# Inversion on diagonal blocks of 64, attention products in halves of 64, and products of constants in TensorE's waits

## The reference, cut to what matters

```python
for layer in range(DEPTH):
    h = rms_norm(x, mix_norm[layer])
    c_rwkv, c_dil, c_mla, c_hgrn = split_cols(h @ w_in[layer], MIXER_COLS)
    y_a = rwkv7_time_mix(c_rwkv, ...)
    y_b = dilated_attention(...)
    y_c = mla_attention(...)
    y_d = hgrn2_mixer(...)
    x = x + jnp.concatenate([y_a, y_b, y_c, y_d], axis=-1) @ w_out[layer]
    h = rms_norm(x, ffn_norm[layer])
    x = x + (swiglu(h, ...) if layer % 2 == 0 else moe_swiglu(h, ...))
return rms_norm(x, final_norm)
```

```python
def step(state, inp):
    r_t, w_t, k_t, v_t, kk_t, a_t = inp
    s_kk = jnp.einsum('bhvk,bhk->bhv', state, kk_t)
    state = (state * w_t[:, :, None, :] - s_kk[..., None] * (kk_t * a_t)[:, :, None, :]
             + v_t[..., None] * k_t[:, :, None, :])
    return state, jnp.einsum('bhvk,bhk->bhv', state, r_t)
```

## Time and profile before

| | us |
|---|---|
| median of 3 runs | 1707.56 (1707.05 to 1708.32) |
| profiled execution | 1705.68 |
| its span, first to last instruction | 1704.1 |
| mean granted TensorE clock | 0.973 of full |
| TensorE busy | 1594.8 (94%) |
| VectorE busy | 1321.5 (78%) |
| ScalarE busy | 1046.3 (61%) |
| GpSimd busy | 147.6 (9%) |
| HBM read and written | 432.54 MB and 23.59 MB, 268 GB/s over the span |

### The profile page before, as it was taken

How to read it: one execution, slowest core, us unless ns; L and a number is a source line. 1 busy time by engine, 2 the same in 40 slices (tenths; PEclk the granted TensorE clock), 3 DMA queues, 4 the chain that set the end, 5 groups by cost and what they waited for, 6 DMA issues and landing times.

```text
span 1704.1 us, 25728 instructions
## 1 busy us (share of the span) xinstructions
PE 1594.8 (94%) x9284; PEld 1373.5 (81%) x9284; DVE 1321.5 (78%) x1204; ACT 1046.3 (61%) x1032; POOL 147.6 (9%) x154
## 2 busy tenths in 40 slices
PE   6888978999897898799999999999999999999997
PEld 6877868999796787778888888888888888888776
DVE  4888555444457875578888898888888888888997
ACT  4634344343444344467777777777777777777775
POOL 1152100000003320000000000000000000000720
PEclk9989998999998999799999999999999999999999
DMA  6429035553242200679999999999999999999992
GB/s 240 162 78 406 27 154 192 179 188 125 74 149 90 75 1 1 265 281 371 382 378 373 364 398 370 376 387 370 385 376 372 389 372 381 381 373 363 401 357 120
DMA packets 67974, 456.88 MB, mean 268 GB/s; under 512 B 7264, under 2 KB 8448, under 8 KB 16464
## 3 DMA queue, kind: packets, MB, share of 16 engines
q1 hardware_dynamic: 59696, 425.28, 64.9%
q0 software_dynamic: 8080, 30.84, 4.7%
q10 hardware_dynamic: 144, 0.05, 0.0%
HBM read 432.54 MB, written 23.59 MB: 268 GB/s over the span
## 4 chain that ended last, share of the span: by engine, by line
PE 78%; DVE 12%; issue 5%; ACT 4%; DMA 0%; DVEq 0%; SPq 0%; ACTq 0%
PE bank L383 32%; PE bank L408 16%; PE bank L1173 8%; PE bank L386 8%; PE bank L636 6%; PE bank L412 4%; DVE wl L458 2%; ACT wh L454 1%; PE bank L668 1%; PE bank L396 1%; DVE ml L623 1%; DVE hs L1927 1%; PE bank L1178 1%; DVE rw L1827 1%; PE bank L1485 1%
## 5 line engine op out<-in xcount | busy, mean ns | idle before, releaser
L458 DVE TENSOR_TENSOR wl<-ring,wh 128x2048 fp32r<-128x2048 f32 x369 | 853.9, 2317 | 181.0 <-ACT wh L454 177.5
L454 ACT ACTIVATE wh<-ring 128x2048 fp32r<-128x2048 f32 x369 | 705.6, 1914 | 120.2 <-PE bank L408 48.8
L383 PE MATMUL bank<-wh,xh 128*128 128x512 f32 x896 | 359.7, 401 | 4.5 <-DVE wl L458 3.0
L383 PE MATMUL bank<-wh,xl 128*128 128x512 f32 x896 | 350.6, 391 | 0.0
L383 PE MATMUL bank<-wl,xh 128*128 128x512 f32 x896 | 349.2, 390 | 0.0
L383 PEld LDWEIGHTS bank<-wh,xh 128*128 128x128 f32 x896 | 168.2, 188 | 37.4 <-DVE wl L458 3.7
L383 PEld LDWEIGHTS bank<-wh,xl 128*128 128x128 f32 x896 | 168.1, 188 | 37.2
L383 PEld LDWEIGHTS bank<-wl,xh 128*128 128x128 f32 x896 | 168.7, 188 | 32.5
L408 PE MATMUL bank<-wh,gh 128*128 128x512 f32 x448 | 176.2, 393 | 5.9 <-DVE gl L531 5.9
L408 PE MATMUL bank<-wl,gh 128*128 128x512 f32 x448 | 175.0, 391 | 0.0
L408 PE MATMUL bank<-wh,gl 128*128 128x512 f32 x448 | 174.9, 390 | 0.0
(11 more groups left out here) (320 smaller groups left out, 2482.1 us busy)
## 6 DMA issues: line engine op xcount, KB each, us to landing
ring<-in_moe_w SPq DMA_DIRECT2D x336, 1024.0 KB, 5.0
ring<-in_ffn_w SPq DMA_DIRECT2D x33, 1024.0 KB, 4.7
ring<-in_w_in SPq DMA_DIRECT2D x24, 1024.0 KB, 4.9
ring<-in_w_out SPq DMA_DIRECT2D x8, 1024.0 KB, 4.7
job_x<-xrow POOLq DMA_DIRECT2D x1, 8192.0 KB, 27.7
job_y<-xrow POOLq DMA_DIRECT2D x1, 8192.0 KB, 46.3
xrow<-job_x POOLq DMA_DIRECT2D x7, 512.0 KB, 9.6
job_y<-yj POOLq DMA_DIRECT2D x7, 512.0 KB, 4.7
```

Source lines behind the costliest of these rows:

```text
L383: ins = nc.tensor.matmul(up_bank(run, par, 0)[:], x[:, 0:C], w[b][:, k], **kw)
L454: nc.scalar.activation(wh[:, buf], flat_slot(slot), ACT.Copy).then_inc(sem("w_high"), 1)
L458: nc.vector.tensor_tensor(wl[:, buf], flat_slot(run.place(i)[0]), wh[:, buf].bitcast(F32), ALU.subtract).then_inc(sem("w_split"), 1)
```

## The change

`BLOCKS` = 6 levels now work on diagonal blocks of `H` = 64 and the last level joins them. A block constant `blocks` (two masks of 64 columns and six level masks, stacked for both diagonal blocks) is loaded on SyncE's queue behind unit 5, in both layers, and counted by `const_in`. The first score set is computed as 24 products of 64x64 instead of 8: the two diagonal blocks of each matrix side by side in the first 256 columns of a bank, the block above the diagonal in the next. VectorE masks the diagonal ones into `atd` and copies the others to `ato`. All tiles of the inversion (`xin`, `xit`, `mtd`, `pid`) are 128x256 per half in place of 128x512; each product of a matrix becomes two of 64x64x64. The transposes into `xin` become products with the identity. In level 6 only X0^T (A01 X1)-like products are left: 4 + 4 per half. Its result goes, negated, to the upper rows of `xit`, and the upper diagonal block is kept in `xi0`. `solve` takes two products a head.

`attend` writes its output in two halves of 64 partitions: 6 products in place of 3. `spin(b, n)` puts n products of the constant `ones` with 256 columns of constants into bank b, whose result nobody reads.

```diff
+        def spin(b, n):
+            for _ in range(n):
+                nc.tensor.matmul(bank[b][:, 0:T], cst("ones"), const[:, 0:T], start=True, stop=True)
...
+                    if u == 5:
+                        sp.dma_start(blocks[:].rearrange("p a b -> p (a b)"), A["blocks"]).then_inc(sem("const_in"), 16)
...
-                for l in range(1, LEVELS):
+                for l in range(1, BLOCKS):
...
-                        settle(nc.gpsimd.tensor_tensor(mtm[:, hv], atm[:, hv], over(lvl(l), 4), ALU.mult), "level_masked")
+                        settle(nc.gpsimd.tensor_tensor(mtd[:, hv], atd[:, hv], over(blocks[:, 2 + l], 4), ALU.mult),
+                               "level_masked")
...
+                        if n == 0:
+                            for to, at, (k0, i0) in ((0, 0, (0, 0)), (H, 0, (H, H)), (0, T, (0, H))):
+                                for half in range(2):
+                                    h, c = 2 * (m // 2) + half, m % 2
+                                    lo, hi, j = rows(h)
+                                    mm(bank[bk + half][to:to + H, at + m * H:at + (m + 1) * H],
+                                       a[lo:hi, j, c * P + k0:c * P + k0 + H], b[lo:hi, j, c * P + i0:c * P + i0 + H],
+                                       sig="chunk_ready" if m == 3 and at and half else None)
+                            continue
...
-                    mm(first, pts[:, n % 2, 0:P], v[:, 0])
-                    mm(second, pts[:, n % 2, P:T], v[:, 0], True, False)
-                    mm(second, pts[:, n % 2, T:3 * P], v[:, 1], False, True, "attended")
+                    for q in (0, P // 2):
+                        mm(first[q:q + P // 2], pts[:, n % 2, q:q + P // 2], v[:, 0])
+                    for q in (0, P // 2):
+                        mm(second[q:q + P // 2], pts[:, n % 2, P + q:P + q + P // 2], v[:, 0], True, False)
+                        mm(second[q:q + P // 2], pts[:, n % 2, T + q:T + q + P // 2], v[:, 1], False, True,
+                           "attended" if q else None)
...
+                DIAGONAL = tuple((m, r, slice(r * H, r * H + H)) for m in range(4) for r in range(2))
...
-                        for m in range(4):
-                            mm(bank[2 + half][:, m * P:(m + 1) * P], mtm[:, 4 * half + m], xin[:, 4 * half + m],
-                               sig="mx_ready" if m == 3 else None)
+                        for m, r, d in DIAGONAL:
+                            if not last:
+                                mm(of_block(bank[2 + half][d], m), mtd[d, 4 * half + m], xin[d, 4 * half + m],
+                                   sig="mx_ready" if m == 3 and r else None)
+                            elif r:
+                                mm(of_block(bank[2 + half][d], m), ato[0:H, 4 * half + m], xin[0:H, 4 * half + m],
+                                   sig="mx_ready" if m == 3 else None)
...
                         beside(l, half)
+                        if last:
+                            spin(4, 1)
...
-                        mm(bank[6][:, h * HD:(h + 1) * HD], xit[:, mat(h, c)], rsol[:, h],
-                           sig="u_ready" if h == NH - 1 else None)
+                        o, m = bank[6][:, h * HD:(h + 1) * HD], mat(h, c)
+                        mm(o[0:H], xi0[0:H, m], rsol[0:H, h])
+                        mm(o[H:P], xit[:, m], rsol[:, h], sig="u_ready" if h == NH - 1 else None)
```

More of the change, by code:

```diff
@@ L144, in constants, with block_constants @@
     return c
+def block_constants():
+    i = np.arange(P)[:, None] % H
+    q = np.arange(H)[None, :]
+    parts = [i < q, i == q]
+    for l in range(BLOCKS):
+        half = 1 << l
+        parts.append((i // (2 * half) == q // (2 * half)) & ((i // half) % 2 == 0) & ((q // half) % 2 == 1))
+    return np.ascontiguousarray(np.concatenate(parts, 1).astype(np.float32))
 def program(nc, A, out):
@@ L220, in program @@
         hs = mx_sb("hs", [P, NM, P])
+        blocks = mx_sb("blocks", [P, 2 + BLOCKS, H])
         sh = wide
@@ L1208, in unit @@
                     pe.wait_ge(sem("unit_copied"), layer * NU + u - 1)
+                if u == 9 and 0 in parts:
+                    spin(b, 6)
                 for part in parts:
@@ L1474, in _ @@
                         if not last:
-                            for m in range(4):
-                                mm(bank[2 + half][:, m * P:(m + 1) * P], xit[:, 4 * half + m], pin[:, 4 * half + m],
-                                   sig="xmx_ready" if m == 3 else None)
-                        for m in range(4):
-                            mm(bank[6 + half][:, m * P:(m + 1) * P], pin[:, 4 * half + m], xit[:, 4 * half + m],
-                               sig="xmx_t_ready" if m == 3 else None)
+                            for m, r, d in DIAGONAL:
+                                mm(of_block(bank[2 + half][d], m), xit[d, 4 * half + m], pid[d, 4 * half + m],
+                                   sig="xmx_ready" if m == 3 and r else None)
+                        for m, r, d in DIAGONAL:
+                            if not last:
+                                mm(of_block(bank[6 + half][d], m), pid[d, 4 * half + m], xit[d, 4 * half + m],
+                                   sig="xmx_t_ready" if m == 3 and r else None)
+                            elif r:
+                                mm(of_block(bank[6 + half][0:H], m), pid[d, 4 * half + m], xit[d, 4 * half + m],
+                                   sig="xmx_t_ready" if m == 3 else None)
                         beside(l, half)
+                        if last:
+                            spin(4, 1)
                 def add(o, l, r, first=False, sig=None):
@@ L1513, in _ @@
                 attend_scores(4)
+                spin(4, 2)
                 solve(0)
@@ L1566, in _ @@
                         norm_part(2 * layer + 1, u - 1)
+                spin(6, 4)
                 norm_part(2 * layer + 1, NO - 1)
+                spin(6, (6, 4)[layer])
                 if layer == 0:
@@ L1747, in _ @@
                             act.wait_ge(sem("xmx_t_ready"), nth(12, 2 * (l - 2) + half))
-                        copy(flat(pin[:, 4 * half:4 * half + 4]), bank[2 + half][:], "pin_ready")
+                        d = slice(H if l == LEVELS - 1 else 0, P)
+                        copy(flat(pid[d, 4 * half:4 * half + 4]), bank[2 + half][d, 0:T], "pin_ready")
                     if 0 <= l - 3 < NH:
@@ L1969, in _, with blocks_of @@
                 tt_(flat(rw[:, BN]), bank[5][:], flat(sh[:, J_V:J_V + 2]), ALU.mult, "bonus_used")
-                for n, (o, mask, sign) in enumerate(((atm, "ups", 1.0), (btm, "ups", 1.0), (ctm, "upi", -1.0),
-                                                     (dtm, "upi", 1.0))):
+                def blocks_of(b, at=0, d=slice(0, P)):
+                    return b[d, at:at + T].rearrange("p (a b) -> p a b", b=H)
+                dve.wait_ge(sem("chunk_ready"), nth(4))
+                for half in range(2):
+                    tt_(atd[:, 4 * half:4 * half + 4], blocks_of(bank[4 + half]), over(blocks[:, 0], 4), ALU.mult)
+                for half in range(2):
+                    settle(nc.vector.tensor_copy(ato[0:H, 4 * half:4 * half + 4],
+                                                 blocks_of(bank[4 + half], T, slice(0, H))),
+                           "chunk_masked" if half else "dve_chain")
+                for half in range(2):
+                    hv = slice(4 * half, 4 * half + 4)
+                    tt_(xit[:, hv], atd[:, hv], over(blocks[:, 2], 4), ALU.mult)
+                    stt(xit[:, hv], xit[:, hv], -1.0, over(blocks[:, 1], 4), ALU.mult, ALU.add, "xit_ready")
+                for n, (o, mask, sign) in enumerate(((btm, "ups", 1.0), (ctm, "upi", -1.0), (dtm, "upi", 1.0)), 1):
                     dve.wait_ge(sem("chunk_ready"), nth(4, n))
```

57 lines of the change are left out of this document (41 added, 16 removed).

## The result

The changed kernel took 1689.64 us (1686.49 to 1691.80 in four runs, the kernel before on the same chip 1707.66). The ratio is 0.9895 with a 95% interval of 0.9882 to 0.9908: faster by 18.0 us where 23.2 were forecast, inside the range. The profiled execution spans 1690.2 us against 1704.1, 13.9 less. The four executions of the changed kernel differ with their mean granted clock: 1691.80 and 1691.31 us at 0.983 and 0.986, 1687.98 and 1686.49 us at 0.990; the profiled one is the slowest.

A forecast was written before the change was run, and what follows sets the result against it. TensorE was taken to bound the mixers and the experts' entry. Two layers -17.6, starts -1.8, router and gather -3.8 sum to -23.2: 1705.68 to 1682.5, plus 1.9 carried over, 1684.4 us; 8 in 10 range 1674 to 1701.

The forecast's parts named there:

- Levels 2 to 5: Middle levels of the inversion: halved block products on TensorE save 2.0 us a level, -8.0 a layer.
- Front: Ahead of the inversion: halved masks and less GpSimd interference bring the first level's query product 1.1 us earlier.
- Level 1: First inversion level: a longer TensorE wait puts part at 1.2 GHz, eating the block products' 0.8 us: 0.
- Level 6: Last inversion level: one block multiplied (-1.7), attention -0.3, shape changes +0.4, three constants +1.3: -0.4 a layer.
- rival C: Inversion: small block products drop the clock to 1.2 GHz, +10 us a layer instead of -9.5, 1723 us; chance 0.06.
- Solve: Behind the inversion: alternating 64x64 and 128x64 products pay shape changes, two solves on the chain, +2.3 us a layer.
- Attention in halves: Attention product within a level: six half products for three, 0.67 to 0.35 us, -0.3 each.
- Fifth output half: Output products behind the inversion: constants in the waits before keep full clock, 4.56 to 2.89 us, -1.7 a layer.
- Norm part: Last norm product of a layer: 1.66 us becomes 1.1, -0.5.
- Starts: Openings of both layers and the dense FFN: constants partly fill the norm wait, -0.6 each, -1.8 for three.
- Router and gather: Entry of the experts: constants keep the clock, router -3.5 + 1.5 = -2, gather 5.47 to 3.6, -1.8; together -3.8.
- bound of -2.8: Openings of both layers and the dense FFN: best end for each place, where -0.6 was booked; other bound +0.5.

The follow-up runs named there:

- no tail: The changed kernel without the five products of constants around the end of the inversion: 1693.74 us, ratio 0.9910 to the kernel before.
- level 1: The changed kernel with six more products of constants ahead of TensorE's wait for the first latent query input: 1684.3 us, ratio 0.9861.
- starts: The changed kernel with longer runs of constants (16, 15 and 13) at the openings of both layers and the dense net: 1682.44 us, ratio 0.9864.
- router: The changed kernel with VectorE's two weight splits behind the routing steps and without the four constants before the selection wait: 1686.21 us, ratio 0.9877.
- the four together: The changed kernel with solves grouped by shape and the edits of level 1, starts and router in one kernel: 1676.12 us, ratio 0.9818.
- the row order: The changed kernel issuing each half's four upper blocks first, then its four lower ones, instead of taking turns: 1699.19 us, ratio 0.9964.

## Why the prediction came out right, and where it did not

- **Levels 2 to 5, -8.0 a layer.** Right. 158.59 to 183.78 is 25.2 us, before 156.69 to 190.25, 33.56: -8.4. The distance of 0.03 from the earlier trace rows was the right one; where the order was spoilt it is 0.043, still under 0.055.
- **Front, -1.1.** The stretch moved as booked (-1.1 and -1.2), in part by luck. From the first scores to the query product, which is what I reasoned about, it is 17.34 us in both layers and 17.99 and 18.00 before: -0.65. The rest came in the projections ahead of it. The first scores themselves were cheaper than booked: 48 products in 1.15 us, 0.020 apart and not 0.029.
- **Level 1, 0.** The mechanism was right and the size was off: the clock did fall behind a wait of 3.03 us, but the cost was +3.5 us in layer 0 and +0.6 in layer 1, not "a gain eaten". Filled, the level gives -0.9. This is most of the 3.7 us missing in layer 0.
- **Level 6, -0.4, and its three constants.** The time was nearly right (4.68 to 4.53 us), the reason not. I booked the five constants around the end of the inversion as a cost of 1.9 us a layer. They hold the clock for the 10 us behind it; without them the stretch behind the first solve is 3.3 to 4.0 us longer, 3.0 a layer when their own time is taken off. The step that failed is rival C: I judged it by the middle levels, where it does not happen, and did not ask it of level 6 and the wait of 1.00 us behind it.
- **Solve, +2.3.** Right to 0.1 us (2.05 us each in the chain), from 0.20 us a change in the earlier trace rows. The Trainium skill (TensorEngine Tiling (Array Packing), Gotcha 1: PSUM Pressure) says that row tiles cannot use one bank at a time; here they did, 32 instructions in 1.15 us, and the measurement decides.
- **Attention in halves, -0.3 each.** Mis-sized: at most 0.18, and nothing that could be seen at the end.
- **Fifth output half, -1.7.** Nearly right in layer 1 (4.61, as the row below shows, to 3.13), not in layer 0 (4.56 to 4.14), where a wait of 2.17 us stands between the two groups of constants and the clock fell again from 229.5 to 232.9 us. **Norm part, -0.5.** Right (1.66 to 1.15 in layer 0, 1.56 to 1.15 in layer 1, in the chain).

```profile
681.09 4.61 PE bank L668 x24
```

- **Starts, -0.6 each.** Nothing at the dense net in this execution: the first set of products behind the wait takes 25.74 us in the chain, as it did before, and its first 5.6 us, 258.02 to 263.60, run at 0.50. Nothing at layer 1 either; there a partial fill is worth nothing or all of the clock, 3 to 4 us, from one profiled kernel to the other, and the even -0.6 had no such either-or. The full fill brought both, as the bound of -2.8 said.
- **Router and gather, -3.8.** The step that failed by as much as level 1. Both products shrank as booked, but I took them to be on the path because TensorE was busy. VectorE's two splits, 4.5 us, stood ahead of the routing in both kernels and hid the whole gain of the router: router to gather takes 15.47 us, before 15.52. The 1.5 us booked against it for the four constants did not come either. In addition ScalarE's second copy starts at 713.79, 1.4 us behind the end of the gather (708.56 + 3.84), which eats most of the gather's 1.6. In five other runs (no tail, level 1, starts, router, and the four together) it came at once, with the same two constants behind the gather. Its cause is open.

The misses lie nearly all on one side: 3.7 in level 1 of layer 0, 3.5 at the router, 1.2 at the dense net and the start of layer 1, 1.7 at the output halves, against 1.1 that the experts gave unasked: about 9 us in the profiled execution. Over the medians it is 5.2, because the profiled execution of the changed kernel (1691.8 us) is the slowest of its four, and that of before (1705.7) was 1.9 under its median. That the sum came out near is partly luck. The blocks' gain was booked as if the clock were held; with no constants it was not, and the time was 1708.0, outside the stated range. Five of the constants that held it were booked as a cost of 3.8 us, and without them the time was 4.1 us longer (intervals that overlap), or 6 by the stretches of the trace.

## What to carry to other kernels

Halving the work of an engine that is the bound can cost it its clock: look for the thinnest step of the new version, the wait next to it and what runs behind, not for the mean of all steps. Test a composite change also without each part; here blocks alone brought nothing, constants alone 6.6 us, and both 18. A filler placed for one version is a cost in another, so the version to compare with needs fillers of its own. Before booking a shorter product, ask which engine ends last behind it: the router's 3.3 us were hidden behind two splits on VectorE, and changing their place gave 2.5 us, as long as the clock was held there.

## What the runs showed of the hardware

- Products of 64x64 in the two diagonal halves of the array ran side by side when they took turns (0.030 us between starts), also into one bank; four and four they took 1.54 us for 32 where turns take 1.15. The 48 products of the first scores, which take turns between row halves and two banks, were 0.020 us apart.
- TensorE did not keep its products in program order: in the run with the row order a `proj,pin` product started at 166.04, ahead of a `pin,proj` one of 166.09 that was issued earlier. The Trainium skill (TensorE: Matmul & The Clock Gate, The mechanism) has products start strictly in program order; this trace shows otherwise.
- A change between 64x64 and 128x64 products costs 0.14 us more than a following product of the same shape (six changes, 0.85 us).
- The same idle time did not always end in the same clock. Behind 3.3 to 3.9 us the granted clock was 0.50 within 1.5 us in all eight such runs at the start of layer 0 and at the dense net; behind 3.33 us at the start of layer 1 it was 0.50 in three of them and 1.00 in five.
- A much shorter wait went with a fall too: in the runs without constants at the end of the inversion, TensorE idled 1.00 us behind the last level and the attention product beside it, and some 10 us of what followed ran at 0.50 in both layers.
